# A hybrid S5/GLA decoder layer: other wait points for PE's first pairs, a written-out PE loop, and small moves on four engines

## The chip, the cores and the metric

The kernel runs on one core of a Trainium2 chip. The metric is the time of one execution in device microseconds (us). A core has five engines that run their own instruction streams side by side and wait for each other on semaphores: PE (TensorE, matrix products into PSUM), DVE (VectorE), ACT (ScalarE), POOL (GpSimd) and SP (SyncE, here a DMA queue). ACT issues DMAs as well. PSUM has eight banks of 512 fp32 columns.

## The reference

One layer of a decoder over 2048 prompt tokens and 8 x 4 new tokens, in fp32, width 1024:

```python
h = rmsnorm(x, g_mix)
z = h @ w_in          # u | q | k | v | r | a_low | gate_s5 | gate_gla
y5 = s5_mixer(u, ...)                       # 32 groups, 64 complex states
z5 = gelu(y5); o5 = z5 * sigmoid(z5 @ w_s5_glu)
og = gla_mixer(q, k, v, log_sigmoid(a_low @ w_gate_up + b_gate) / 16, ...)
og = rmsnorm_per_head(og) * g_gla_norm * silu(r)
m = sigmoid(gate_s5) * (o5 @ w_s5_br) + sigmoid(gate_gla) * (og @ w_gla_br)
x = x + m @ w_out
x = x + relu(rmsnorm(x, g_ffn) @ w_ff1) ** 2 @ w_ff2
y = rmsnorm(x, g_final)
```

## The kernel before

Activations lie feature-major: a tile is 128 features by all tokens of a half. The tokens are cut in two halves; the first has 1024 prompt tokens in two blocks of 512 columns, the second 1024 prompt tokens and all 32 new ones in three blocks of 352. Each half runs the whole layer, one after the other.

To keep fp32 accuracy, every operand is split in a high and a low part, and each product is three matmuls (`three`, lines 589 to 591): high x high, high weight x low, low weight x high. Weights come in blocks of 128 x 512 (four 128 x 128 pieces). SP loads a block into one of 2 raw buffers when POOL has split the block two earlier; POOL makes the high and low part (`split`, lines 571 and 573) in one of 4 places, in order 0, 1, 2, 3, when PE has finished with that place (`w_used`); PE waits for `w_split` of the place. SP's queue also carries, between the loads, the constants (`first_loads`) and the gates that come back from DRAM.

PE writes a product either in a set of banks (set 0: banks 0 to 2, set 1: banks 3 to 5) or, for the jobs in between ("dense": keys, inputs, gates, branch products), block by block in banks 6 and 7 by turns. Before PE starts a tile in a set it waits for the set's reader (`set_free`, semaphores `set0_read` and `set1_read`). In a stage such as the output product or the feed-forward part, `tile_pair` makes a tile in set 0 and then one in set 1. The first two tiles of a stage go through `first_pair` instead (from line 653): the right-hand tiles k = 0 to 7 are just being made by ACT and DVE (`split_ready` counts DVE's low parts), so the pair goes over k in the outer loop and over the two sets in the inner one:

```python
for s in range(2):
    set_free(half, s, stage, 0)
for n in range(2):
    for s in range(2):
        pe.wait_ge(w_split[2 * s + n], it + 1)
    for q in range(4):
```

It is used for the queries (`SP_X`), the output product (`SP_MG`) and the feed-forward part (`SP_H2`), in each half.

The start: ACT squares the eight input tiles as they land, DVE adds the squares (line 1650), PE sums them over the features (`row_sums`, line 644), ACT makes the root, DVE scales, ACT and DVE split, and PE's first pair begins.

After the values' products PE transposes each value tile (`values`, lines 722 and 724) and ACT copies it out (`values_out`, lines 1292 and 1294). Between `values(2)` and `values(3)` stands a whole gate tile ("gs", 0). Then the GLA chunks begin with `gla_keys` (line 735), which waits for all four value tiles.

In the branches (`branches` on DVE and ACT) PE makes GLA branch tiles ("bg"), the S5 gate's products ("glu") and the S5 branch ("bs") in the order of `D_JOBS`. DVE multiplies each "bg" block by its gate (`gla_block`), which frees the bank, and makes the low part of the S5 output z (`z_low`), for which it waits for ACT's rounded high part. The gates were stored in DRAM and come back on SP's queue (`gla_gate_back`, line 476; semaphores `gg_landed`). PE waits for all four low parts before "glu".

The feed-forward part has 8 groups of "up" and "down" products; three turns of a register loop on PE (line 1094), ACT and DVE make groups 2 to 7. In the second half `ff_last` makes the last group's final four tiles block by block (4 tiles x 12 matmuls a block), so that the final norm can start on block 0: DVE adds each piece to the residual, ACT squares it, DVE adds squares, PE sums them (`last_sums`, lines 911 and 913, one tile into the second piece of the next block), ACT makes the root (`root_block`, lines 1551 and 1554), DVE scales eight pieces (`scale_block`, line 2372) and SP stores four tiles at a time (lines 556 and 558).

## Time and profile before

| | |
|---|---|
| time, median of 3 runs | 2885.11 us (2884.95 to 2885.32) |
| the profiled execution's own time | 2883.77 us |
| its span | 2881.6 us |
| PE busy | 2816.3 us (98%) |
| PE weight loads busy | 2532.0 us (88%) |
| DVE busy | 1323.2 us (46%) |
| POOL busy | 1168.8 us (41%) |
| ACT busy | 502.3 us (17%) |

The span is what the trace covers; the execution's own time has some 2 us around it. Lines such as L589 are lines of the kernel before; most DVE operations have the line of a helper (L1650), so they are told apart by their tiles: `f_` names a fp32 view of a region, `r_` the rounded view of the same memory, `ps` is PSUM. Matmuls overlap, and their ends are modelled.

### The profile page before, as it was taken

The page shows a single profiled execution, that of the slowest core. Times are in us where ns is not written, and L with a number is a line of the kernel's source. Part 1 is how long each engine was busy: PE and PEld are TensorE (multiplying, and loading weights), DVE is VectorE, ACT ScalarE, POOL GpSimd, SP SyncE. Part 2 cuts the span into 40 slices and gives each one's busy share as a digit, 9 for nine tenths or more (in the row PEclk, how much of TensorE's full clock was granted, in tenths as well). Part 3 has the DMA queues.
Part 4 walks back from the last instruction along what each step waited for, and adds up shares of the span by engine and source line. Part 5 has one row for each costly group of instructions (what it writes and reads, how often), then busy time and mean ns, then how long its engine had stood idle before and what let it go on. Part 6 is the DMA issues. An engine that isn't in the chain of part 4 may idle for free.

```text
span 2881.6 us, 40391 instructions
## 1 busy us (share of the span) xinstructions
PE 2816.3 (98%) x16170; PEld 2532.0 (88%) x16170; DVE 1323.2 (46%) x2039; ACT 502.3 (17%) x731; POOL 1168.8 (41%) x917
## 2 busy tenths in 40 slices
PE   6999999999999999999999999999999999999997
PEld 4778888887888888888899999999999999999997
DVE  7845657364433333234723556666444223332235
ACT  3222221412100000001222223142120000000002
POOL 4433432544544444444444332244444443344441
PEclk9999999999999999999999999999999999999999
DMA  4333244531111111113113333563211111111112
GB/s 144 118 96 88 67 132 154 186 99 52 48 48 48 49 48 48 48 48 108 48 54 123 76 84 100 169 211 100 71 42 47 48 45 45 48 45 48 45 48 75
DMA packets 122999, 230.48 MB, mean 80 GB/s; under 512 B 15280, under 2 KB 43728, under 8 KB 122704
## 3 DMA queue, kind: packets, MB, share of 16 engines
q1 hardware_dynamic: 79312, 150.16, 17.3%
q10 hardware_dynamic: 43520, 77.83, 8.5%
q8 instruction: 137, 2.24, 0.3%
q14 instruction: 30, 0.25, 0.0%
HBM read 183.85 MB, written 44.09 MB: 79 GB/s over the span
## 4 chain that ended last, share of the span: by engine, by line
PE 94%; DVE 3%; ACT 1%; DVEq 1%; issue 1%; ACTq 0%; DMA 0%
PE ps L589 29%; PE ps L591 29%; PE ps L590 29%; PE ps L753 1%; PE ps L838 1%; PE ps L871 1%; PE ps L784 0%; DVE f_h L1650 0%; PE ps L865 0%; DVE f_m L1650 0%; DVE f_g L1650 0%; DVE f_z L2372 0%; PE ps L762 0%; DMA s_constants<-f_m 0%; PE ps L644 0%
## 5 line engine op out<-in xcount | busy, mean ns | idle before, releaser
L571 POOL TENSOR_TENSOR w_hi<-w_raw,zero 128x512 fp32r<-128x512 f32 x456 | 536.0, 1175 | 1607.8 <-PE ps L591 1593.7
L589 PE MATMUL ps<-r_h,w_hi 128*128 128x352 f32 (+1 forms) x2352 | 817.7, 348 | 14.2 <-DVE r_h L1650 5.5
L591 PE MATMUL ps<-r_h,w_lo 128*128 128x352 f32 (+1 forms) x2352 | 816.0, 347 | 0.0
L590 PE MATMUL ps<-r_o,w_hi 128*128 128x352 f32 (+1 forms) x1968 | 679.5, 345 | 0.0
L573 POOL TENSOR_TENSOR w_lo<-w_raw,w_hi 128x512 fp32r<-128x512 f32 x456 | 634.7, 1392 | 64.8
L589 PE MATMUL ps<-r_z,w_hi 128*128 128x352 f32 (+1 forms) x1440 | 516.4, 359 | 3.4 <-issue 3.4
L591 PE MATMUL ps<-r_z,w_lo 128*128 128x352 f32 (+1 forms) x1440 | 514.5, 357 | 0.0
L590 PE MATMUL ps<-r_h,w_hi 128*128 128x512 f32 (+1 forms) x1352 | 499.3, 369 | 0.0
L589 PEld LDWEIGHTS ps<-r_h,w_hi 128*128 128x128 f32 x2352 | 442.9, 188 | 52.5 <-issue 14.5
L591 PEld LDWEIGHTS ps<-r_h,w_lo 128*128 128x128 f32 x2352 | 442.9, 188 | 32.2
L590 PE MATMUL ps<-r_m,w_hi 128*128 128x352 f32 (+1 forms) x1240 | 421.2, 340 | 0.0
L590 PEld LDWEIGHTS ps<-r_o,w_hi 128*128 128x128 f32 x1968 | 370.9, 188 | 28.5 <-issue 0.5
L589 PEld LDWEIGHTS ps<-r_z,w_hi 128*128 128x128 f32 x1440 | 271.6, 189 | 36.7 <-issue 6.9
L591 PEld LDWEIGHTS ps<-r_z,w_lo 128*128 128x128 f32 x1440 | 271.6, 189 | 27.7
L590 PEld LDWEIGHTS ps<-r_h,w_hi 128*128 128x128 f32 x1352 | 255.3, 189 | 39.2 <-issue 0.5
L2236 DVE SCALAR_TENSOR_TENSOR f_g<-ps,f_e 128x1024 f32<-128x1024 f32 (+1 forms) x64 | 79.4, 1241 | 394.0 <-PE ps L591 394.0
L1650 DVE TENSOR_TENSOR f_z<-f_z,ps 128x1056 f32<-128x1056 f32 (+1 forms) x104 | 103.8, 999 | 311.7 <-PE ps L591 311.6
L590 PEld LDWEIGHTS ps<-r_m,w_hi 128*128 128x128 f32 x1240 | 233.0, 188 | 13.6
L1650 DVE TENSOR_TENSOR f_h<-f_h,ps 128x1024 f32<-128x1024 f32 (+1 forms) x102 | 108.4, 1063 | 293.3 <-PE ps L591 291.8
L1650 DVE TENSOR_TENSOR f_g<-f_g 128x1024 f32<-128x1024 f32 (+2 forms) x110 | 191.8, 1756 | 8.4
L591 PE MATMUL ps<-r_m,w_lo 128*128 128x512 f32 x384 | 151.6, 395 | 0.0
L589 PE MATMUL ps<-r_m,w_hi 128*128 128x512 f32 x384 | 150.5, 392 | 0.1
(323 smaller groups left out, 2398.4 us busy)
## 6 DMA issues: line engine op xcount, KB each, us to landing
w_raw<-wpack SPq DMA_DIRECT2D x456, 256.0 KB, 2.6
f_z<-s_constants ACTq DMA_DIRECT2D x16, 514.0 KB, 4.9
f_h<-s_constants ACTq DMA_DIRECT2D x16, 514.0 KB, 5.3
f_h<-xT ACTq DMA_DIRECT2D x16, 512.0 KB, 4.2
gate_s_scratch<-f_m ACTq DMA_DIRECT2D x8, 528.0 KB, 3.5
gate_gla_scratch<-f_m ACTq DMA_DIRECT2D x8, 528.0 KB, 3.5
f_z<-gate_s_scratch SPq DMA_DIRECT2D x8, 528.0 KB, 5.4
f_o<-xT ACTq DMA_DIRECT2D x4, 1040.0 KB, 7.8
```

The costliest lines, as they stand in the source:

```text
L571: pool.tensor_tensor(w_hi[:, s, :], raw, zero[:, :].to_broadcast([P, WB]), ALU.subtract)
L573: pool.tensor_tensor(w_lo[:, s, :], raw, w_hi[:, s, :].bitcast(F32), ALU.subtract).then_inc(w_split[s], 1)
L589: pe.matmul(out, wh, h, start=first, stop=False)
L590: pe.matmul(out, wh, l, start=False, stop=False)
L591: return pe.matmul(out, wl, h, start=False, stop=last)
L753: last = pe.matmul(ps[0:L - LEVELS[l], 2 * (col // 512) + h % 2, col % 512:col % 512 + L // 2], fa[rows, at:at + L - LEVELS[l]], right, st ...
L838: last = pe.matmul(ps[64 * g:64 * g + 64, 4 + t % 2, q * uc:(q + 1) * uc], fv(QKV[half] + C_SLOT[r] + c0 + 64 * g, 64), fv(WORK[half] + (t ...
L871: last = pe.matmul(out(t, g), fa[rows(g), at(t) + c0:at(t) + c0 + P], fa[rows(g), st:st + yc], start=False, stop=q == 1)
L1650: return dve.tensor_tensor(out, a, b, op)
L2236: dve.scalar_tensor_tensor(cols(half, r), psum_cols(half, q % 2), 0.0, cols(half, ft(half, E_NORM)), ALU.max, ALU.mult).then_inc(set_read[ ...
```

## The change

- `first_pair`, for `SP_H2` in both halves and for `SP_X` in the second: PE waits for set 0 alone, takes k = 0 to 3 in set 0, then waits for set 1 and takes k = 0 to 3 there; k = 4 to 7 as before.
- PE's loop over the feed-forward groups is a Python loop: its instructions are written out.
- `ff_last` waits for set 1 only ahead of its fourth tile; `last_sums` of a block comes after the first piece of the next block, ACT's `root_block` ahead of that block's squares; DVE scales the block before in two halves, behind its adds of pieces 2 and 3; SP stores two tiles at a time.
- POOL waits for the first sums (`ssum_ready`) before the second of the first four splits.
- PE makes one block of ("gs", 0), then `values(3)`, then the other blocks; ACT follows.
- DVE makes two GLA tiles, then the S5 low parts by turns with the blocks of the next two; PE waits for the low parts of "glu" and "bs" one by one.

```diff
             for s in range(RING):
+                if s == 1:
+                    pool.wait_ge(ssum_ready, 1)
                 split(s, 0)
...
             def first_pair(half, stage, it, split, hi, lo, between=None):
-                for s in range(2):
+                alone = split == SP_H2 or (split == SP_X and half > 0)
+                for s in range(1 if alone else 2):
                     set_free(half, s, stage, 0)
                 for n in range(2):
+                    if alone and n == 0:
+                        for s in range(2):
+                            if s:
+                                set_free(half, s, stage, 0)
+                            pe.wait_ge(w_split[2 * s], it + 1)
+                            for k in range(4):
+                                pe.wait_ge(split_ready, half * SP_ALL + split + k + 1)
+                                last = tiles_of(half, s, k, KT_D, w_hi[:, 2 * s, k * P:(k + 1) * P],
+                                                w_lo[:, 2 * s, k * P:(k + 1) * P], hi, lo)
+                            last.then_inc(w_used[2 * s], 1)
+                        if between:
+                            between()
+                        continue
...
-                for s in range(2):
-                    set_free(half, s, "ff", ff_set(g, "down") + LAST // 2)
+                set_free(half, 0, "ff", ff_set(g, "down") + LAST // 2)
...
                         if b == 0:
+                            if x == RING - 1:
+                                set_free(half, 1, "ff", ff_set(g, "down") + LAST // 2)
...
-                        if b and x == 1:
+                        if b and x == 0:
                             last_sums(half, b - 1)
...
-                dense_tile(half, ("gs", 0), x_hi, x_lo)
+                dense_block(half, ("gs", 0), 0, x_hi, x_lo)
                 values(half, 3)
+                for b in range(1, NB[half]):
+                    dense_block(half, ("gs", 0), b, x_hi, x_lo)
...
+                    elif m == 0:
+                        dense(half, (kind, 0), 0, 0, z_hi, z_lo, SP_Z5 if kind == "glu" else SP_O5)
+                        for b in range(1, NB[half]):
+                            dense_block(half, (kind, 0), b, z_hi, z_lo)
                     else:
-                        if m == 0:
-                            pe.wait_ge(split_ready, half * SP_ALL + (SP_Z5 if kind == "glu" else SP_O5) + KT_S)
                         dense_tile(half, (kind, m), z_hi, z_lo)
...
-                with pe.Fori(0, FF_GROUPS // 2 - 1) as i:
+                for i in range(FF_GROUPS // 2 - 1):
...
                 for b, (c0, cn) in enumerate(BLK[half]):
+                    if b:
+                        root_block(b - 1)
                     for x in range(RING):
...
-                        if b and x == 1:
-                            root_block(b - 1)
...
                 gla_branch(0)
+                gla_branch(1)
                 z_low(0)
-                gla_branch(1)
-                z_low(1)
-                z_low(2)
-                gla_branch(2)
-                z_low(3)
-                gla_branch(3)
+                for m in (2, 3):
+                    dve.wait_ge(gg_landed[m], (half + 1) * 16)
+                    gla_block(m, 0)
+                    z_low(2 * m - 3)
+                    for b in range(1, NB[half]):
+                        gla_block(m, b)
+                    if m == 2:
+                        z_low(2)
...
-                        last.then_inc(ssum_ready, 1)
-                        if b:
-                            scale_block(b - 1)
-                    scale_block(NB[half] - 1)
+                            if x == RING - 1:
+                                last.then_inc(ssum_ready, 1)
+                            if b and x >= 2:
+                                scale_block(b - 1, range((x - 2) * RING, (x - 1) * RING))
+                    scale_block(NB[half] - 1, range(KT_D))
```

How the order moves, at three places. PE at the start of the feed-forward part's first pair in the first half (`r_m`, `r_h_57`: the output product's right-hand sides; `r_z`, `r_o`: high and low part of the feed-forward input; in brackets the semaphores waited for). Before:

```order
L589 MATMUL ps<-r_m,w_hi 128x512
L590 MATMUL ps<-r_h_57,w_hi 128x512
L591 MATMUL ps<-r_m,w_lo 128x512
L589 MATMUL ps<-r_z,w_hi 128x512 [waits w_split2,w_split0,split_ready,set1_read,set0_read]
L590 MATMUL ps<-r_o,w_hi 128x512
```

Now:

```order
L592 MATMUL ps<-r_m,w_hi 128x512
L593 MATMUL ps<-r_h_57,w_hi 128x512
L594 MATMUL ps<-r_m,w_lo 128x512
L592 MATMUL ps<-r_z,w_hi 128x512 [waits split_ready,w_split0,set0_read]
L593 MATMUL ps<-r_o,w_hi 128x512
```

The waits for place 2 and for set 1 have left the first product; they stand at the product 24 matmuls later.

DVE in the second half's branches (`f_o<-f_g,ps` and `f_o<-f_o,ps`: GLA blocks, three to a tile; `r_m<-f_h_49,r_h_57`: an S5 low part). Before:

```order
L1650 TENSOR_TENSOR f_o<-f_g,ps 128x352 x3
L1650 TENSOR_TENSOR r_m<-f_h_49,r_h_57 128x1056
L1650 TENSOR_TENSOR f_o<-f_o,ps 128x352 x3
L1650 TENSOR_TENSOR r_m<-f_h_49,r_h_57 128x1056 x2
L1650 TENSOR_TENSOR f_o<-f_o,ps 128x352 x3
L1650 TENSOR_TENSOR r_m<-f_h_49,r_h_57 128x1056
L1650 TENSOR_TENSOR f_o<-f_o,ps 128x352 x3
```

Now:

```order
L1675 TENSOR_TENSOR f_o<-f_g,ps 128x352 x3
L1675 TENSOR_TENSOR f_o<-f_o,ps 128x352 x3
L1675 TENSOR_TENSOR r_m<-f_h_49,r_h_57 128x1056
L1675 TENSOR_TENSOR f_o<-f_o,ps 128x352
L1675 TENSOR_TENSOR r_m<-f_h_49,r_h_57 128x1056
L1675 TENSOR_TENSOR f_o<-f_o,ps 128x352 x2
L1675 TENSOR_TENSOR r_m<-f_h_49,r_h_57 128x1056
L1675 TENSOR_TENSOR f_o<-f_o,ps 128x352
L1675 TENSOR_TENSOR r_m<-f_h_49,r_h_57 128x1056
L1675 TENSOR_TENSOR f_o<-f_o,ps 128x352 x2
```

Six GLA blocks now stand ahead of the first low part, and each later low part behind a single block or a pair.

DVE at the end, from the second block's last piece on (`f_z<-f_z,ps`: a piece's add; `f_h_49`: squares added; `f_z<-f_z,vec,f_e`: a scaled piece). Before:

```order
L2372 SCALAR_TENSOR_TENSOR f_z<-f_z,vec,f_e 128x352 x8
L1650 TENSOR_TENSOR f_z<-f_z,ps 128x352 x2
L1650 TENSOR_TENSOR f_h_49<-f_h_49 128x352
L1650 TENSOR_TENSOR f_z<-f_z,ps 128x352
L1650 TENSOR_TENSOR f_h_49<-f_h_49 128x352
L1650 TENSOR_TENSOR f_z<-f_z,ps 128x352
L1650 TENSOR_TENSOR f_h_49<-f_h_49 128x352
L2372 SCALAR_TENSOR_TENSOR f_z<-f_z,vec,f_e 128x352 x16
```

Now:

```order
L2401 SCALAR_TENSOR_TENSOR f_z<-f_z,vec,f_e 128x352 x4
L1675 TENSOR_TENSOR f_z<-f_z,ps 128x352 x2
L1675 TENSOR_TENSOR f_h_49<-f_h_49 128x352
L1675 TENSOR_TENSOR f_z<-f_z,ps 128x352
L1675 TENSOR_TENSOR f_h_49<-f_h_49 128x352
L2401 SCALAR_TENSOR_TENSOR f_z<-f_z,vec,f_e 128x352 x4
L1675 TENSOR_TENSOR f_z<-f_z,ps 128x352
L1675 TENSOR_TENSOR f_h_49<-f_h_49 128x352
L2401 SCALAR_TENSOR_TENSOR f_z<-f_z,vec,f_e 128x352 x12
```

Eight of the last sixteen scalings have moved ahead, four before the last piece's add and four behind its squares' sum. In all, PE's order has 10302 rows before and 14092 now.

## Rows read from the trace of the kernel before

**Rows 1.** The page's first part: busy us (share of the span) x instructions

```profile
PE 2816.3 (98%) x16170; PEld 2532.0 (88%) x16170; DVE 1323.2 (46%) x2039; ACT 502.3 (17%) x731; POOL 1168.8 (41%) x917
```

**Rows 2.** Waits of PE: engine, line, whom; us in total, times, longest

```profile
PE ps L589 <- issue: 8.8, 6, 2.0
...
PE ps L735 <- ACT f_z L1292: 1.4, 1, 1.4
PE ps L735 <- ACT f_e L1294: 1.3, 1, 1.3
```

**Rows 3.** Timeline of PE, loop turns, second half: start, us, operation [idle before <-releaser]

```profile
2397.86 0.32 PE L590 MATMUL ps<-r_m,w_hi 128*128 128x352 f32 x1
2398.01 0.32 PE L591 MATMUL ps<-r_h,w_lo 128*128 128x352 f32 x1
2400.06 0.43 PE L589 MATMUL ps<-r_h,w_hi 128*128 128x352 f32 x1 [1.72 <-issue]
...
2585.59 0.42 PE L589 MATMUL ps<-r_h,w_hi 128*128 128x352 f32 x1 [0.93 <-issue]
```

**Rows 4.** The chain that ended last, first 32 us: start, us, engine and line

```profile
12.71 1.23 DVE f_h L1650
...
20.18 2.14 DVE f_h L1650
...
22.45 3.77 PE ps L644 x4
...
31.66 0.76 PE ps L589
```

**Rows 5.** Timeline of ACT: the last input tile's square

```profile
17.26 1.06 ACT L1178 ACTIVATE f_h<-f_h 128x1024 f32<-128x1024 f32 x1 [0.17 <-DMA f_h<-xT]
```

**Rows 6.** Groups by line, POOL: busy us, mean ns of one | idle before

```profile
L573 POOL TENSOR_TENSOR w_lo<-w_raw,w_hi 128x512 fp32r<-128x512 f32 x456 | 634.7, 1392 | 64.8
L571 POOL TENSOR_TENSOR w_hi<-w_raw,zero 128x512 fp32r<-128x512 f32 x456 | 536.0, 1175 | 1607.8 <-PE ps L591 1593.7 <-DMA w_raw<-wpack 13.9
```

**Rows 7.** Timeline of PE: first products of three first pairs

```profile
710.90 0.47 PE L589 MATMUL ps<-r_z,w_hi 128*128 128x512 f32 x1 [1.36 <-issue]
...
1425.99 0.40 PE L589 MATMUL ps<-r_z,w_hi 128*128 128x352 f32 x1 [2.04 <-issue]
...
2119.24 0.40 PE L589 MATMUL ps<-r_h,w_hi 128*128 128x352 f32 x1 [1.40 <-issue]
```

**Rows 8.** Timeline of DVE: reads of set 0 and set 1 before the first pair

```profile
698.51 1.22 DVE L1650 TENSOR_TENSOR f_h<-f_h,ps 128x1024 f32<-128x1024 f32 x1 [6.43 <-PE ps L591]
...
709.58 1.22 DVE L1650 TENSOR_TENSOR f_h<-f_h,ps 128x1024 f32<-128x1024 f32 x1 [6.42 <-PE ps L591]
```

**Rows 9.** Timeline of PE: first product of the last group's four tiles

```profile
2840.69 0.40 PE L589 MATMUL ps<-r_o,w_hi 128*128 128x352 f32 x1 [1.39 <-issue]
```

**Rows 10.** Timeline of ACT: copies of the fourth value tile, first half

```profile
218.19 1.08 ACT L1292 ACTIVATE f_z<-ps 128x512 f32<-128x512 f32 x2 [0.47 <-PE ps L722]
```

**Rows 11.** Timelines of DVE and PE in the second half's branches

```profile
1914.51 1.26 DVE L1650 TENSOR_TENSOR r_m<-f_h,r_h 128x1056 fp32r<-128x1056 f32 x1 [3.63 <-ACT r_h L1496]
...
1916.25 0.43 PE L589 MATMUL ps<-r_h,w_hi 128*128 128x352 f32 x1 [2.09 <-DVE f_o L1650]
...
1923.49 0.43 PE L589 MATMUL ps<-r_h,w_hi 128*128 128x352 f32 x1 [1.23 <-DVE f_o L1650]
```

**Rows 12.** The gates' tile, 1913 to 1915 us: issues, and us from issue to landing

```profile
L476 SPq DMA_DIRECT2D f_o<-gate_gla_scratch x2: 430/430/430, 1913.4 to 1913.8; - x2
...
DMA to landing us min/median/max: 6.1/6.5/7.0
```

**Rows 13.** Timeline of DVE: the last scalings

```profile
2868.68 8.12 DVE L2372 SCALAR_TENSOR_TENSOR f_z<-f_z,vec,f_e 128x352 f32<-128x352 f32 x16
```

**Rows 14.** Busy time from 2872 to 2880: PE, PEld, DVE, ACT, POOL, clock, DMA, GB/s

```profile
2872.00:2880.00 8.00, 0.00 (x0) 0.00 (x0) 4.78 (x10) 0.70 (x2) 0.00 (x0) 0.50 1.03 345
```

More of the change, by code:

```diff
@@ L550, in _ @@
             for b, (c0, cn) in enumerate(BLK[half]):
-                for k in range(0, KT_D, RING):
-                    sp.wait_ge(y_ready, KT_D + 2 * b + k // RING + 1)
-                    y = fv(X_HI[half] + k * W, RING * W).rearrange("p (k n) -> p k n", n=W)
+                for k in range(0, KT_D, 2):
+                    sp.wait_ge(y_ready, KT_D + 4 * b + k // 2 + 1)
+                    y = fv(X_HI[half] + k * W, 2 * W).rearrange("p (k n) -> p k n", n=W)
                     own = min(cn, N - c0)
-                    out = [yT[h, :, k * N:(k + RING) * N].rearrange("p (k n) -> p k n", n=N) for h in range(HALVES)]
+                    out = [yT[h, :, k * N:(k + 2) * N].rearrange("p (k n) -> p k n", n=N) for h in range(HALVES)]
                     sp.dma_start(out[half][:, :, c0:c0 + own], y[:, :, c0:c0 + own]).then_inc(y_stored, 16)
@@ L1633, in _ @@
                 exps(half, 1)
-                for b in range(NB[half]):
+                gate_out(half, 0, 0)
+                values_out(half, 3)
+                for b in range(1, NB[half]):
                     gate_out(half, 0, b)
-                values_out(half, 3)
                 gla(half)
@@ L1643, in _ @@
             act.wait_ge(s5dec_stored, 32)
-            act.wait_ge(y_stored, 16 * (KT_D + 2 * NB[1] + 2))
+            act.wait_ge(y_stored, 16 * (KT_D + 4 * NB[1] + 4))
         @block.vector
@@ L2189, in branches @@
                 gla_branch(0)
+                gla_branch(1)
                 z_low(0)
-                gla_branch(1)
-                z_low(1)
-                z_low(2)
-                gla_branch(2)
-                z_low(3)
-                gla_branch(3)
+                for m in (2, 3):
+                    dve.wait_ge(gg_landed[m], (half + 1) * 16)
+                    gla_block(m, 0)
+                    z_low(2 * m - 3)
+                    for b in range(1, NB[half]):
+                        gla_block(m, b)
+                    if m == 2:
+                        z_low(2)
                 for m in range(KT_S):
@@ L2365, in last_square, with scale_block @@
                                   ALU.add)
-                    def scale_block(b):
+                    def scale_block(b, tiles):
                         c0, cn = BLK[half][b]
                         dve.wait_ge(root_ready, NORM[half]["y"] + b + 1)
-                        for k in range(KT_D):
+                        for k in tiles:
                             y = ft(half, X_HI[half], k)[:, c0:c0 + cn]
@@ L2373, in scale_block @@
                                                             ft(half, E_NORM)[:, c0:c0 + cn], ALU.mult, ALU.mult)
-                            if k % RING == RING - 1:
+                            if k % 2:
                                 last.then_inc(y_ready, 1)
```

## The prediction

> **What bounds the kernel now.** Start with the busy table: PE (TensorE) works 2816.3 of 2881.6 us [rows 1]. No other engine comes near, so time is won only where PE stands idle, 65 us in all. Next read who makes PE wait: of that list the change touches the entry "issue" with 8.8 us in 6 places, two waits for ACT at the GLA keys (1.4 and 1.3 us) [rows 2], and the starts and the end that follow below. "Issue" says only that no releaser was seen; the timeline around each place tells what it was. In the list and in the timeline a matmul's end is modelled: in 352-column blocks matmuls start every 0.16 us (2397.86, 2398.01) and show 0.32 [rows 3], so an idle time printed in brackets is about 0.16 us shorter than what PE lost. I add 0.16 to each PE gap between matmuls of the three-product kind.
>
> **The start (GpSimd's wait).** DVE adds eight squared tiles. The third add runs 1.23 us; the last, beside GpSimd's weight splits, 2.14, and PE's first sums follow it at 22.45 [rows 4]. With three of the four splits held until the sums are there, five adds from 12.71 at about 1.3 each would be through at 19.2. ACT's last square ends at 17.26 + 1.06 = 18.32 [rows 5], and one add of 1.23 behind it ends at 19.6. So the sums come 22.32 - 19.6 = 2.7 us sooner. The fourth weight load now waits for the second split, so 256 KB less stand before the input's last tiles, which then come a little sooner; I take **3.0 us**, from 2.7 as the lower bound without that. What is late next: three splits of 1.18 + 1.39 = 2.57 us by the means [rows 6] run from 19.3 and end by 27.0; PE's pair needs the places 0 and 2, so two of the held splits, 24.5. PE's first product, now at 31.66 [rows 4], would be at 28.7. Four us of room. SP's queue is held too: behind the fourth load stand the constants, masks and S5 tables (`first_loads`), which go out some 5 us later; PE asks for the constants before the same product, and the rest is used only after the input's eight tiles.
>
> **First pairs.** PE waits for both bank sets before the first product: idle 1.36, 2.04 and 1.40 us [rows 7]. The second set's reader is DVE's add, 709.58 + 1.22 = 710.80, and PE goes on at 710.90; the first set was read from 698.51 on [rows 8]. The change asks for set 1 only after half of set 0's product, 4 tiles x 2 blocks x 3 matmuls x 0.23 = 5.5 us later (4 x 3 x 3 x 0.16 = 5.8 in the second half), when that add is long done. Low parts of tiles 0 to 3 are ready long before, and the number of products is the same. Gain 4.80 + 3 x 0.16 = **5.3 us**. It costs nothing as long as place 2's split is done 5.5 us after place 0's; GpSimd does them in the order 0, 1, 2, and had both before.
>
> **PE's loop written out.** In the second half the loop's two turns cost 1.72 and 0.93 us [rows 3]; in the first half no turn is among the six. Gain 2.65 + 2 x 0.16 = **3.0 us**. No operation is added or taken away; what stands against the term is the first rival below.
>
> **Last group.** Before its last four tiles PE waits for both sets, 1.39 us [rows 9]; set 1 is then needed only by the fourth tile, 3 x 12 x 0.16 = 5.8 us on. Gain **1.5 us**. DVE is behind on the first of these blocks, but has caught up when PE asks for the first sums.
>
> **Values before the rest of the gate.** PE's keys wait 1.37 and 1.31 us (1.4 and 1.3 in the list [rows 2]) for ACT's copies of the fourth value tile, which begin at 218.19 and end 1.1 us later [rows 10]. With one gate block before these transposes and the others behind, the copies have at least 3.8 us of PE work to hide under. Gain **2.7 us**. ACT's key copy then comes behind the last gate block, but PE has a gate product between.
>
> **S5's low parts in turn.** DVE's first low part stands 3.63 us waiting for ACT's rounded tile, and the GLA blocks behind it in the queue hold PE's banks: PE loses 2.09 and, at the next such place, 1.23 us [rows 11]. With two GLA tiles first, and then a low part behind each one's first block, DVE never waits long: 2.09 + 1.23 + 0.32 = 3.6 us. But the wait is not gone: the third gate tile's load is issued at 1913.4 and the fourth's at 1913.8, and they land 6.1 and 7.0 us later [rows 12], the third at 1919.5 at the earliest. PE, no longer held, finishes that tile's first block about 1917.7 (the held block would have begun at 1916.25 - 2.09 - 0.16 = 1914.0, and a block is 12 x 0.16 = 1.92 us) and needs its bank again at 1919.8; DVE's product ends near 1920.2. I take 0.6 off: **3.0 us** (1.4 if the load is a us later and DVE chases it, 3.6 at best). In the first half PE did not wait here, and the new order leaves it so. The wait per tile instead of four changes nothing: the last low part is done before PE is there.
>
> **The tail.** Roots move up by a tile, and block 1's scaling goes in two halves behind DVE's adds of tiles 2 and 3. Good: in the profile, DVE scales sixteen pieces without a break from 2868.68, 8.12 us [rows 13], the stores of both blocks leave together, and the DMA engines are full from 2872 to 2880 at 345 GB/s [rows 14], over 3 us past DVE's last piece. With block 1's stores earlier, and two-tile stores (0.35 MB, 1.0 us at that rate), the end follows the last piece by about 1.2 us less. Bad: four scalings, 4 x 0.51 = 2.0 us, now stand before DVE's last add, and the last root comes later by an estimated 0.7 us; PE also waits a little for the middle block's sums. Net **0.5 us**, between -0.7 and 1.2.
>
> **Sum.** 3.0 + 5.3 + 3.0 + 1.5 + 2.7 + 3.0 + 0.5 = 19.0 us. The profiled execution took 2883.77 us (span 2881.6), so 2864.8; the median of the runs shown, 2885.11, is 1.34 above it. I forecast 2866.1 for the median.
>
> **Rivals.**
> - *Written-out code starves PE* (slower). The PE program grows from 10302 to 14092 rows of the order; if PE met a fetch stall where it now enters new code, each costing what a turn costs (1.72 us [rows 3]), at each of the 24 up and down parts that the loops held, that is 41 us: 2866.1 + 41 = 2907. From 15 such stalls on (25 us) the change is slower by more than 0.2%. For it: only the loop's turns show such idle time. Against it: over half of PE's time is spent in straight code already, and the six places of "issue" are three first pairs, two turns and the last group [rows 2, 3, 7, 9]. 3%. The Trainium skill, Runtime: NRT & Kernel Launch, Instruction fetch mechanics, says that an engine's instructions are fetched ahead in sequence, and that a taken branch to a place not yet fetched stalls. By that rule the turns' gain is kept whole and this rival doesn't occur; the trace agrees in that the straight parts show no such row, and differs in that the first half's turns, branches too, show none either.
> - *The start gives its gain back.* The held splits run on beside DVE's later steps, and DVE's operations of that kind take 1.23 alone and 2.14 beside a split [rows 4]. If the splits slip by 2 us, they meet the first scaling and low part, and the 3.0 go: 2869. The Trainium skill, SBUF — State Buffer, Who interferes with whom, has GpSimd and DVE exclude each other for a whole instruction; by it such a meeting costs either one up to the other's full length. 10%.
> - *The next wait is close behind.* The gaps at the first pairs, the last group and the S5 branch close only in part, because DVE and ACT, which now feed an earlier PE, are themselves the limit; half of 5.3 + 1.5 + 3.0 is lost: 2871. For it: PE's second wait in the S5 branch follows the first by 7 us [rows 11]. Against it: at the first pairs DVE has only one add left. 12%.
> - *The change doesn't do it.* "Issue" at the first pairs and the last group is not the set's wait but a cost of the place itself (a code change, the weights' split), and stays: 2866.1 + 6.8 = 2873. Against it: PE goes on 0.10 us after DVE's add [rows 7, 8]. 4%.
>
> **How the numbers follow.** My forecast has 71%, these four 29%. The sum's upper bounds (3.3, 5.5, 3.4, 1.6, 2.7, 3.6, 1.2) give 21.3 us, that is 2864; rounding up for the restart of PE after each closed gap, 2862. The lower ones (2.0, 4.0, 2.0, 1.0, 2.0, 1.4, 0) give 12.4 and 2873, which takes in three of the rivals. A measurement of this kernel tells about 0.2%, 5.8 us, from no change. All cases but the written-out stream, and some mishap that I don't see, lie beyond it: faster 92%, same 4%, slower 4%.
>
> **What would show it.** In the changed profile: DVE's adds all near 1.23 us and PE's first sums near 19.5; no idle row at the three first pairs, the loop's turns and the last group; PE's keys without a wait; in the second half's GLA branch at most one wait, of under 1 us, whose cause is the gate's load. At the end the DMA engines should not be full when DVE's last piece is done, and the last root should come later against PE's last product. I am wrong if new "issue" rows stand inside the feed-forward part, or if PE waits for a split or for low parts after the first pairs' first set.

## The result, and the profile after

The changed kernel takes **2861.53 us** (median of four executions, 2860.50 to 2865.04) beside 2885.22 us for the kernel before: ratio 0.9918, 95% interval 0.9901 to 0.9935. It is faster, by more than the 19.0 us of the sum: the median is half a microsecond below the range of 2862 to 2873. Five further executions of the same kernel have a median of 2863.11 us (below), inside the range, so the half microsecond itself is within the spread. The profiled execution took 2860.5 us with a span of 2858.6, 23.0 us shorter than the span before.

The first part of the changed kernel's page answers to [rows 1]: PE has the same 16170 matmuls in 5.4 us less of busy time, so a part of the gain is not idle time at all: some 3 us of it are the lower clock below.

```profile
PE 2810.9 (98%) x16170; PEld 2529.5 (88%) x16170; DVE 1324.5 (46%) x2039; ACT 502.5 (18%) x731; POOL 1165.6 (41%) x917
```

All waits of PE in the changed kernel (line, whom it waited for, us in total, times, longest). Against [rows 2] the entry "issue" and the two waits at the keys are gone. L592 is now what L589 was, L753 what L735 was.

```profile
PE ps L647 <- DVE f_h L1675: 19.4, 1, 19.4
PE ps L592 <- DVE r_h L1675: 6.8, 1, 6.8
PE ps L883 <- DVE f_m L2130: 3.3, 2, 2.5
PE ps L929 <- DVE f_h L1675: 2.8, 2, 2.3
PE ps L592 <- DVE f_o L1675: 1.3, 1, 1.3
PE ps L771 <- ACT khT L1375: 1.3, 1, 1.3
PE ps L740 <- ACT f_z L1287: 1.0, 1, 1.0
PE ps L706 <- DVE f_z L1882: 1.0, 1, 1.0
PE ps L883 <- DVE f_o L2130: 0.7, 1, 0.7
```

PE's timeline in the changed kernel at the six places of [rows 3, 7, 9] (first pairs, loop turns, last group): the product starts with no idle time in brackets.

```profile
704.64 0.39 PE L592 MATMUL ps<-r_z,w_hi 128*128 128x512 f32 x1
...
1417.02 0.32 PE L592 MATMUL ps<-r_z,w_hi 128*128 128x352 f32 x1
...
2101.90 0.32 PE L592 MATMUL ps<-r_h,w_hi 128*128 128x352 f32 x1
...
2380.73 0.32 PE L592 MATMUL ps<-r_h,w_hi 128*128 128x352 f32 x1
2565.05 0.32 PE L592 MATMUL ps<-r_h,w_hi 128*128 128x352 f32 x1
...
2818.49 0.32 PE L592 MATMUL ps<-r_o,w_hi 128*128 128x352 f32 x1
```

PE does the same matmuls in nearly the same order, so the gain can be followed: take the start of one matmul before, less its start after. At the second first pair that is 1425.99 - 1417.02 = 8.97 us so far. By place, in us, each read once the difference is steady again behind the place:

| place | forecast | profiled |
|---|---|---|
| start, at the first product | 3.0 | 31.66 - 29.94 = 1.7 |
| values, both halves | 2.7 | 1.6 + 1.5 = 3.1 |
| PE at a lower clock near 434 us | none | 1.5 |
| three first pairs | 5.3 | 1.6 + 2.3 + 1.6 = 5.5 |
| PE at a lower clock behind the second | none | 1.5 |
| loop, with 0.4 in the first half | 3.0 | 0.4 + 2.0 + 1.2 = 3.6 |
| S5's low parts | 3.0 | 2.3 + 1.4 = 3.7 |
| last group | 1.5 | 1.6 |
| tail | 0.5 | 0.7 |
| rest | | 0.1 |

The two lower clocks are seen in the windows of the kernel before (columns: PE, PEld, DVE, ACT, POOL busy, granted clock, DMA share, GB/s). PE is busy throughout. The first window stands at 0.50, which is the level of 1.2 GHz and not of 2.4; the second, at 0.66 in the mean, reaches beyond such a stretch on both sides:

```profile
1427.50:1430.50 3.00, 3.00 (x12) 3.00 (x12) 3.00 (x3) 2.27 (x3) 0.00 (x0) 0.50 0.58 161
433.00:438.00 5.00, 5.00 (x41) 4.46 (x42) 0.18 (x1) 0.60 (x1) 0.00 (x0) 0.66 0.16 34
```

The same work in the changed kernel:

```profile
1417.00:1421.00 4.00, 4.00 (x26) 3.98 (x25) 4.00 (x3) 0.93 (x1) 2.85 (x2) 1.00 0.14 53
431.00:435.00 4.00, 4.00 (x41) 3.36 (x41) 1.84 (x7) 0.60 (x1) 0.00 (x0) 1.00 0.48 153
```

At the start the sums come at 19.38 us, close to the 19.5 of the prediction, but the first product only 1.7 us sooner. DVE's timeline in the changed kernel shows the step between them: the angle steps, which the prediction doesn't name, take from 19.15 to 27.74 us.

```profile
19.15 0.17 DVE L1724 TENSOR_SCALAR f_o<-f_o 128x16 f32<-128x16 f32 x1
...
19.47 0.91 DVE L1675 TENSOR_TENSOR f_o<-f_o 128x16 f32<-128x16 f32 x1
20.31 2.64 DVE L1729 TENSOR_SCALAR f_e<-f_e 128x16 f32<-128x16 f32 x8
23.03 1.24 DVE L1732 TENSOR_SCALAR f_e<-f_e 128x144 f32<-128x144 f32 x1
24.34 0.23 DVE L1734 TENSOR_SCALAR f_e<-f_e 128x144 f32<-128x144 f32 x1
24.66 2.78 DVE L1737 SCALAR_TENSOR_TENSOR f_e<-f_e 128x144 f32<-128x144 f32 x3
...
27.66 1.41 DVE L2293 SCALAR_TENSOR_TENSOR f_h<-f_h,vec,f_g 128x512 f32<-128x512 f32 x2
```

GpSimd's held splits at that time, in its timeline:

```profile
22.91 1.26 POOL L573 TENSOR_TENSOR w_lo<-w_raw,w_hi 128x512 fp32r<-128x512 f32 x1
24.44 1.04 POOL L571 TENSOR_TENSOR w_hi<-w_raw,zero 128x512 fp32r<-128x512 f32 x1 [0.27 <-DMA w_raw<-wpack]
25.62 1.27 POOL L573 TENSOR_TENSOR w_lo<-w_raw,w_hi 128x512 fp32r<-128x512 f32 x1
```

DVE's operation at 23.03 ends at 24.27, just behind GpSimd's at 22.91 + 1.26 = 24.17; the next one falls into GpSimd's pause and takes 0.23. The Trainium skill, SBUF — State Buffer, Who interferes with whom, lets one of the two engines hold the shared pair of ports for a whole instruction; these rows agree. ACT's root was ready by 25.18 + 1.06 = 26.24:

```profile
25.18 1.06 ACT L1167 ACTIVATE f_g<-f_g 128x1024 f32<-128x1024 f32 x1
```

### The profile page after: what moved, and what is told of

Read it like the earlier page. It is cut to its first block, busy times and chain, and to the rows that moved or that the text cites. A ratio compares the mean times of both kernels' runs of the same rounds, so it can differ in the third digit from the quotient of the medians.

```text
span 2858.6 us, 40302 instructions
## 1 busy us (share of the span) xinstructions
PE 2810.9 (98%) x16170; PEld 2529.5 (88%) x16170; DVE 1324.5 (46%) x2039; ACT 502.5 (18%) x731; POOL 1165.6 (41%) x917
## 4 chain that ended last, share of the span: by engine, by line
PE 95%; DVE 3%; DMA 1%; DVEq 1%; ACT 0%; issue 0%; ACTq 0%
PE ps L594 29%; PE ps L592 29%; PE ps L593 29%; PE ps L771 1%; PE ps L856 1%; PE ps L889 1%; PE ps L883 1%; PE ps L802 0%; PE ps L780 0%; DMA s_constants<-f_m 0%; DVE f_m L1675 0%; PE ps L813 0%; DMA f_h<-xT 0%; DVE f_g L1675 0%; DVE f_h L1675 0%; PE ps L987 0%
## 5 line engine op out<-in xcount | busy, mean ns | idle before, releaser
L592 PE MATMUL ps<-r_h,w_hi 128*128 128x352 f32 (+1 forms) x2352 | 817.5, 348 | 8.2 <-DVE r_h L1675 6.8
L592 PE MATMUL ps<-r_z,w_hi 128*128 128x352 f32 (+1 forms) x1440 | 515.6, 358 | 0.0
L592 PEld LDWEIGHTS ps<-r_h,w_hi 128*128 128x128 f32 x2352 | 442.9, 188 | 45.2 <-issue 11.0
L592 PEld LDWEIGHTS ps<-r_z,w_hi 128*128 128x128 f32 x1440 | 271.0, 188 | 32.6 <-issue 2.7
L592 PE MATMUL ps<-r_m,w_hi 128*128 128x512 f32 x384 | 150.3, 391 | 0.0
```

The source lines that it names most:

```text
L592: pe.matmul(out, wh, h, start=first, stop=False)
```

## The experiments

Theory after the result: the gain is the sum of closed gaps, plus the end of a lower clock that followed one of them, less 1.35 us lost where the held splits meet DVE's angle steps. Single executions of one program differ by several us here (2860.50 to 2865.04 above), so medians of four or five tell little about 1 us. What follows is read from the start of the same matmul in two traces; "the changed kernel" is the profile above. Together with the two profiles above, 18 profiles are compared.

### The start

```diff
 for s in range(RING):
-    if s == 1:
-        pool.wait_ge(ssum_ready, 1)
     split(s, 0)
```

> The changed kernel with GpSimd's one new wait (for the first row sums) taken out; all else stays. Theory: the wait buys the first sums 3.07 us (22.45 to 19.38 us) and costs 1.35 us of them, because the three held splits now run beside DVE's angle steps (8.6 us instead of 3.2). Without it the first sums return to 22.3 to 22.6 us, the angle steps to 3.2 us, the first product to 31.5 to 31.8 us (29.94 with the wait), and the time rises by 1.7 us. Rival, the earlier sums come from something else (arrival of the input): the sums stay near 19.4 us without the wait, the first product comes near 28.6 us, and the time falls by about 1.3 us.

Measured: median 2864.3 us; first sums at 22.56, first product at 31.77. DVE's angle steps, in this kernel's timeline:

```profile
22.64 0.17 DVE L1673 TENSOR_TENSOR f_o<-f_o 128x16 f32<-128x16 f32 x1
22.74 0.70 DVE L1727 TENSOR_SCALAR f_e<-f_e 128x16 f32<-128x16 f32 x8
23.52 0.23 DVE L1730 TENSOR_SCALAR f_e<-f_e 128x144 f32<-128x144 f32 x1
...
24.15 1.07 DVE L1735 SCALAR_TENSOR_TENSOR f_e<-f_e 128x144 f32<-128x144 f32 x3
...
29.48 1.42 DVE L2291 SCALAR_TENSOR_TENSOR f_h<-f_h,vec,f_g 128x512 f32<-128x512 f32 x2 [3.95 <-ACT f_g L1165]
```

The same operations without splits beside them: 0.70 us for eight that took 2.64, and DVE waits 3.95 us for the root. The wait moves the sums by 3.2 us and the first product by 1.8; the sums' gain is the wait's.

```diff
-    trig_angles()
     norm_root(NORM[0]["x"], A_G)
 ...
     for k in range(1, KT_D + 1):
         input_tile(0, k)
+    trig_angles()
```

> The changed kernel with GpSimd's wait kept and DVE's angle steps moved from between the first sums and the first scaling to behind the eight input tiles (ScalarE's sine, which reads them, comes later still). Theory: the angle steps beside the held splits were the only thing that gave back part of the earlier sums; the first scaling starts at the end of ScalarE's root, near 26.3 us (27.66 before this edit), the first product near 28.6 us (29.94), and the time falls by 1.3 us. Rival, the start gives its gain back in whatever DVE does beside the splits: the first scaling and the first low part grow by what the angle steps lost, the first product stays between 29.5 and 30.0 us and the time does not move.

Measured: median 2862.22 us. With the sums at 19.59, the first scaling starts when the root is done, and the first product comes at 29.18, 0.76 us sooner:

```profile
26.52 1.79 DVE L2292 SCALAR_TENSOR_TENSOR f_h<-f_h,vec,f_g 128x512 f32<-128x512 f32 x2 [7.07 <-ACT f_g L1167]
```

Measured from the sums, 0.97 of the 1.35 us come back; the other 0.38 go to the rival, since the scaling beside the last held split takes 1.79 instead of 1.41. The median doesn't show it: PE waits 0.4 us more for the S5 kernel's tables (near 145 us) and 1.1 us at a gate (below). Whether the later place of the angle steps causes the first of these isn't shown: the wait is 0.98 us in the changed kernel's profile and 1.55 in a second one of the same kernel, against 1.39 here.

The third is both edits together:

> Both edits at once: no wait of GpSimd, and the angle steps behind the input tiles. Theory: with the sums at 22.3 to 22.6 us the root ends near 29.3 us and the angle steps were done long before it, so that their place is worth nothing here: first product 31.4 to 31.8 us, as with the angle steps in their old place. The wait is then worth 3.0 us with the angle steps out of the way and 1.7 us with them in the way. Rival, the angle steps cost by themselves and not through the splits: the first product comes 1.3 us earlier here too, near 30.3 us.

Measured: first product at 31.77 us, the same as with the angle steps in their old place, so they cost nothing by themselves. (One execution, 2867.69 us; behind the product PE loses 2 us more at the S5 kernel's tables, and some to longer stretches of lower clock near 35, 155 and 1775 us.)

```diff
-    if s == 1:
+    if s == 2:
         pool.wait_ge(ssum_ready, 1)
```

> The changed kernel with GpSimd's wait for the first row sums ahead of its third split instead of its second. The second then runs from 6.0 to 8.5 us, ahead of VectorE's first add (9.8 us), and only two splits (4.8 us) are left to run beside the angle steps. Theory: the sums stay at 19.4 us; the angle steps do some 1.8 us of their 3.2 us of work while the splits run (8.6 us beside them against 3.2 alone) and end near 25.6 us, ahead of ScalarE's root (26.2); the first scaling starts at the root's end, 26.3 us, and the first product comes at 28.6 us (29.94), so that PE is 1.3 us earlier. Rival, the shared work is GpSimd's own queue and not the place: the angle steps still end behind 27 us and PE gains less than 0.4 us.

Measured: sums at 20.15 us, 0.77 later than in the changed kernel. All squares of the input end later here; over the thirteen profiles with the wait the sums lie between 19.0 and 20.3. The first product comes at 29.36, 9.21 us behind the sums instead of 10.56: 1.35 us are back, all of what the splits took. DVE in this kernel:

```profile
21.08 2.64 DVE L1729 TENSOR_SCALAR f_e<-f_e 128x16 f32<-128x16 f32 x8
...
25.42 1.07 DVE L1737 SCALAR_TENSOR_TENSOR f_e<-f_e 128x144 f32<-128x144 f32 x3
...
27.07 1.41 DVE L2293 SCALAR_TENSOR_TENSOR f_h<-f_h,vec,f_g 128x512 f32<-128x512 f32 x2 [0.27 <-ACT f_g L1167]
```

The first eight still meet a split, the last three don't, and DVE is ready 0.27 us ahead of the root. Median 2862.6 us.

### The first pairs, and the clock behind a gap

```diff
-alone = split == SP_H2 or (split == SP_X and half > 0)
+alone = False
```

> The changed kernel with the first pairs at three places (the feed-forward's in both halves, the query's in the second) put back to turns between the two bank sets. Theory: PE's gaps of 1.36, 2.04 and 1.40 us come back, with the lesser ones beside them 5.3 us in all, and PE's steps before and behind those places are as in the changed kernel, so that the time rises by 5.3 us. The term was put at 5.3; the two profiles differed by 7.2 us at the three places, because in the kernel before the granted clock also stood at 0.5 for 3.4 us behind the longest gap, which cost another 1.9. If that fall belongs to the gap it comes back too, at about 1417 us, and the time rises by 7.2 us. Rival, the fall is a matter of the single run: the gaps come back without it. Second rival, the gaps were shifted work that comes back elsewhere: the time rises by under 3 us.

Measured: median 2870.09 us, 8.6 above the changed kernel's. PE's entry "issue" is back with 4.8 us in 3 places; PE loses 1.6, 2.3 and 1.6 us there, and another 1.5 behind the second, where the granted clock is at 0.50 again. The window in this kernel, behind its gap:

```profile
1423.00:1426.00 3.00, 3.00 (x11) 3.00 (x12) 3.00 (x2) 0.91 (x1) 0.94 (x1) 0.50 0.29 85
```

Sum 7.0 of the 7.2 expected. Another 1.9 us of this profile stand at 429 to 436 us, again at 0.50, and 1.2 us behind PE's last sums. Whether either fall belongs to the change one profile can't tell; three more bear on it, two of the kernel before, and one with the pairs put back:

> The kernel before, profiled again. Theory: the granted clock falls to 0.5 again behind the gap of 2.04 us at 1426 us, for about 3.4 us, and costs PE some 1.6 to 1.9 us there; near 434 us it may or may not fall. Rival, the fall at 1427 us was chance: it is absent here, and the gap costs its 2.04 us alone.

> The kernel before, a third profile. Theory: as in the second, a granted clock of 0.5 behind the gap at 1426 us. Rival: none there.

> The changed kernel with the first pairs put back, a second profile. Theory: a granted clock of 0.5 behind the gap near 1422 us again, with or without one near 432 us. Rival: none there.

Measured: 2887.24, 2884.73 and 2870.99 us. Each has the fall behind the gap. The windows, of the second profile of the kernel before, then of the third, then of the pairs put back:

```profile
1427.50:1430.00 2.50, 2.50 (x10) 2.50 (x10) 2.50 (x3) 1.41 (x2) 0.00 (x0) 0.51 0.39 118
```

```profile
1427.50:1430.00 2.50, 2.50 (x10) 2.50 (x9) 2.50 (x3) 1.31 (x2) 0.04 (x1) 0.50 0.40 110
```

```profile
1423.00:1426.00 3.00, 3.00 (x11) 3.00 (x12) 3.00 (x2) 1.03 (x2) 0.82 (x1) 0.50 0.31 87
```

So the fall at the second first pair stands in all five profiles that have the gap, and in none of the thirteen that haven't: it belongs to the gap, and its 1.5 us to the change. The other, near 434 us, follows a wait of 2.53 us at the S5 rows, the same in all 18 (L883 in the list above), that no edit here touches. It stands in 10 of the 18, among them the changed kernel run again (below), so one program does both. That the kernel before has it in three of three leaves open whether the change makes it rarer. A third such stretch, near 1490 us, comes in five of the 18, for 1.5 us each time.

Nor does every gap of that length bring a fall. In the second profile of the kernel before PE's wait in the S5 branch [rows 11] is followed by one too, and costs 1.5 us more than the wait:

```profile
1918.35 0.66 PE L589 MATMUL ps<-r_h,w_hi 128*128 128x352 f32 x1 [2.22 <-DVE f_o L1650]
```

```profile
1918.50:1921.00 2.50, 2.50 (x9) 2.50 (x10) 0.22 (x1) 2.47 (x4) 0.00 (x0) 0.50 0.91 311
```

The same wait is 2.09 and 2.25 us in the other two profiles of that kernel, and 2.35 in the run with the low parts put back (below), and no fall follows it there: one in four, where the first pair has five in five.

### The loop, the S5 low parts, the values, the last group

```diff
-for i in range(FF_GROUPS // 2 - 1):
+with pe.Fori(0, FF_GROUPS // 2 - 1) as i:
```

> The changed kernel with PE's feed-forward loop as a counted loop again. Theory: the turns cost what the kernel before shows, two of 1.72 and 0.93 us in the second half with what follows them and 0.4 us in the first: 3.0 to 3.6 us more, in PE's idle time put down to nothing that the profile shows, and no other change. Rival, the written-out code costs PE something all along (waiting for its instructions) that the gain hides: with the loop back the stretches between the turns run faster and the time rises by less than 1.5 us.

Measured: median 2865.40 us. PE's waits show "issue" with 2.8 us in 2 places, and PE loses 1.8 and 1.6 us at the two turns, none in the first half, and nothing between the turns: 3.4 us. (In the kernel before, a turn of the first half lost 0.4.) Timeline of PE:

```profile
2382.80 0.43 PE L592 MATMUL ps<-r_h,w_hi 128*128 128x352 f32 x1 [1.51 <-issue]
```

```profile
2568.69 0.42 PE L592 MATMUL ps<-r_h,w_hi 128*128 128x352 f32 x1 [1.29 <-issue]
```

The written-out code costs nothing that could be seen. The Trainium skill, Runtime: NRT & Kernel Launch, Instruction fetch mechanics, names a taken branch to a place not yet fetched as what stalls; in this run the second half's turns show idle time, the first half's turns and the straight code none.

```diff
 gla_branch(0)
+z_low(0)
 gla_branch(1)
-z_low(0)
-for m in (2, 3):
...
+z_low(1)
+z_low(2)
+gla_branch(2)
+z_low(3)
+gla_branch(3)
```

(with PE's one wait for four low parts, as before.)

> The changed kernel with VectorE's order in the branches and PE's waits for the S5 low parts put back. Theory: PE's waits of 2.09 and 1.23 us come back in the second half (near 1905 and 1912 us) with 0.2 to 0.4 us in the first half, so that PE is 3.0 to 3.7 us later behind them, and the time rises by as much. Rival, the gates' transfers: VectorE's new order waits for the third gate, and in the changed kernel that landing ends a wait of VectorE's of 1.45 us, so that PE is released by it with under 0.5 us to spare; put back, the order hides this, and the rise is under 2 us.

Measured: median 2866.12 us; PE loses 2.6 and 1.3 us, 3.9 in all and a little over what was expected, and nothing in the first half. Its rows answer to [rows 11]:

```profile
1904.28 0.43 PE L592 MATMUL ps<-r_h,w_hi 128*128 128x352 f32 x1 [2.35 <-DVE f_o L1673]
1911.52 0.43 PE L592 MATMUL ps<-r_h,w_hi 128*128 128x352 f32 x1 [1.22 <-DVE f_o L1673]
```

```diff
-dense_block(half, ("gs", 0), 0, x_hi, x_lo)
+dense_tile(half, ("gs", 0), x_hi, x_lo)
 values(half, 3)
-for b in range(1, NB[half]):
-    dense_block(half, ("gs", 0), b, x_hi, x_lo)
```

(and ACT's copies likewise.)

> The changed kernel with the last values behind the whole first gate tile on PE and ScalarE again, as before the change. Theory: each half loses 1.3 to 1.7 us at the values (near 217 and 925 us of the first half's and second half's values), PE waiting for ScalarE's copies, and the time rises by 2.7 to 3.0 us. Rival, VectorE's first differences and products set the pace there and not the values' copies: the loss is under 1 us in each half.

Measured: median 2866.88 us; PE's waits at L753 come back with 1.4 and 1.3 us, and PE is 1.6 and 1.5 us later behind them: 3.1, as between the two profiles above. That is a little over what was expected, and over the term's 2.7, which took the printed waits as they stand.

```diff
-set_free(half, 0, "ff", ff_set(g, "down") + LAST // 2)
+for s in range(2):
+    set_free(half, s, "ff", ff_set(g, "down") + LAST // 2)
```

> The changed kernel with PE's wait for the second bank set put back ahead of the last group's first tile. Theory: PE's gap of 1.39 us ahead of that group comes back, PE is 1.4 to 1.7 us later behind it, and the end is as much later. Rival, the wait for the second set only moves the gap three tiles on in the changed kernel: PE loses under 0.5 us.

Measured: the gap is back with 1.40 us, and PE is 1.6 us later behind it. (One execution, 2868.26 us; lower clocks cost it 2.7 us from 429 to 436 and 1.5 near 1491.)

### The gate's transfer, the tail, and all together

DVE's timeline in the changed kernel shows what lies behind the S5 gain: its block of the third gate tile starts when the gate's transfer lands, not when PE is done. The two gates' loads in the changed kernel answer to [rows 12]:

```profile
L476 SPq DMA_DIRECT2D f_o<-gate_gla_scratch x2: 430/431/432, 1901.6 to 1902.1; - x2
...
DMA to landing us min/median/max: 5.4/5.9/6.4
```

```profile
1907.11 0.52 DVE L1675 TENSOR_TENSOR f_o<-f_o,ps 128x352 f32<-128x352 f32 x1 [1.45 <-DMA f_o<-gate_gla_scratch]
```

```diff
     for j in range(J): ...
+    gla_gate_back(half, 2)
     sp.wait_ge(yrow3_stored, (half + 1) * 16 * J)
```

(and the same gate is skipped at its later place.)

> The changed kernel with one transfer of SyncE's queue moved: the third GLA gate is fetched between the stores of the last S5 tile and the wait for them, not behind the fetch of that tile and one weight block. Theory: in the changed kernel the landing of that gate ends VectorE's wait ahead of its block (1.45 us near 1907 us), with PE held 0, 0.41 and 1.08 us behind it in three runs; the queue stands idle there for over 1 us, so that the gate lands some 4 us earlier, VectorE's block waits for PE alone, and PE has no wait there in any run: 0 to 1.1 us. Rival, the transfer delays the last S5 tile, whose parts PE then waits for: 0.5 to 2 us more of waiting behind 1908 us, and slower.

Measured: median 2861.37 us. The block now waits 0.30 us, for PE, and PE doesn't wait near 1908 us. (A wait of 1.33 us near 1950 us, later in these branches, stands in all 18 profiles.) DVE's row:

```profile
1906.54 0.52 DVE L1678 TENSOR_TENSOR f_o<-f_o,ps 128x352 f32<-128x352 f32 x1 [0.30 <-PE ps L597]
```

Twelve profiles have the change's order without this edit. PE isn't held in five, the changed kernel's among them, and is held by 0.21 to 1.08 us in seven, by 0.51 in the changed kernel run again. In the five the third gate lands 5.1 to 5.6 us after its issue, in the seven 5.6 to 6.6. So the wait that the prediction expected is there, at 0 to 1.1 us, and it follows the gate's landing.

```diff
-if b and x >= 2:
-    scale_block(b - 1, range((x - 2) * RING, (x - 1) * RING))
+if b:
+    scale_block(b - 1, range(KT_D))   # behind all four x
```

> The changed kernel with the early root of the last tiles and the stores of two tiles kept, but DVE's eight scalings of one column block all behind the next block's last sum, as in the kernel before. Theory: in the changed kernel DVE's add of the last piece waits 1.2 us behind four scalings (2843.9 to 2845.9 us) while PE's last sums wait 2.34 us and DVE itself idles 2.00 us for the last root; with the scalings behind, the last square starts 1.2 us earlier, the idle 2.00 us is filled by the scalings, and DVE's last scaling ends 1.0 us earlier: the time falls by 0.8 to 1.2 us. Rival, the stores set the end: DVE ends earlier but the sixteen scaled pieces then leave in a row, and the time falls by less than 0.3 us or not at all.

In the changed kernel DVE goes like this at the end (four scalings, the last add, four more, then 2.00 us idle):

```profile
2843.91 2.06 DVE L2401 SCALAR_TENSOR_TENSOR f_z<-f_z,vec,f_e 128x352 f32<-128x352 f32 x4
2845.90 0.51 DVE L1675 TENSOR_TENSOR f_z<-f_z,ps 128x352 f32<-128x352 f32 x1
...
2851.01 4.06 DVE L2401 SCALAR_TENSOR_TENSOR f_z<-f_z,vec,f_e 128x352 f32<-128x352 f32 x8 [2.00 <-ACT f_e L1578]
```

Measured with the scalings behind: PE's wait for the last sums falls from 2.34 to 1.23 us, and the sixteen scalings run without a break, as in [rows 13]:

```profile
2848.62 8.12 DVE L2401 SCALAR_TENSOR_TENSOR f_z<-f_z,vec,f_e 128x352 f32<-128x352 f32 x16
```

PE's wait of 0.42 us for the middle block's sums, in the 2.8 us of the list above, is gone too. Against the changed kernel PE was 3.45 us late ahead of these sums (stretches of lower clock and the gate's wait), 1.68 us late at the last sums, and the span ends 2.10 us late: the tail is 1.35 us shorter, a little more than expected. 0.4 us of PE's 1.8 are lost again behind PE's last sums; that the stores, which now leave with less between them, are the cause isn't shown. The median, 2863.81 us, doesn't show the gain. The tail's other parts, the earlier root and the stores of two tiles, were not put back one by one.

The wait ahead of the third split, the early gate and this edit, in one kernel, beside the changed kernel itself once more, on one chip:

> Three edits on the changed kernel at once: the wait ahead of the third split, the early gate, and the scalings of one block behind the last sum of the next. Theory: the places are far apart and PE carries each gain on: 1.3 us at the start, 0 to 1.1 us at the gate, 0.8 us at the end, 2.1 to 3.2 us in all, so 2858.5 to 2859.5 us as the median against 2861.5 us. Rival, the gains are taken back by later waits or by the granted clock: 2861 us or more.

> The changed kernel itself once more, for a time beside that of the three edits and for which parts of the trace repeat. Theory: the waits repeat within 0.3 us, and so does the absence of a lower granted clock near 1417 us, where the gap is gone; a lower clock near 434 us comes in some runs and not in others, since the wait in front of it is the same in both kernels, and shifts a run by 1.3 us; the median lies between 2860.5 and 2863 us. Rival, the fall near 434 us is the kernel before's own: it is absent here again.

Measured: 2862.83 us (2858.66 to 2863.52, ratio 0.9918, 0.9905 to 0.9932) against 2863.11 us (2861.31 to 2864.84, ratio 0.9920, 0.9906 to 0.9933). Each edit does its part in the trace: the first product 9.20 us behind the sums, the gate's block waiting 0.30 us for PE, PE's last wait 1.23 us and the tail 1.2 us shorter. But the time of the whole isn't shown to be shorter. The three edits' profile lost 2.7 us near 434 us, that of the changed kernel again 1.4, at the lower clock, and each 1.5 more near 1490 us (windows near 434 us of the three edits, then of the changed kernel again):

```profile
431.00:435.00 4.00, 4.00 (x33) 3.55 (x34) 0.00 (x0) 0.60 (x1) 0.00 (x0) 0.50 0.14 19
```

```profile
431.00:435.00 4.00, 4.00 (x34) 3.40 (x33) 0.55 (x2) 0.60 (x1) 0.00 (x0) 0.57 0.38 84
```

That one program has this stretch in one execution and not in another is the rest of the answer on the 1.5 us near 434 us: they are in the difference of the two profiles, and that they belong to the change isn't shown.

## Why the prediction was wrong in size

The direction, the places, and the forecast's case were right: no fetch stall came, all six places of "issue" closed, the new wait in the S5 branch stayed small. The time was 4.6 us too high, half a microsecond out of the range. That it fell just outside is chance, as the five further executions show; that the sum was too low is not: the places of the change are worth 21.4 us in the profiles and not 19.0. The step that failed is the size put on closed gaps: 7.0 and not 5.3 us at the first pairs, 3.7 and not 3.0 in the S5 branch, 3.6 and not 3.0 at the loop, 3.1 and not 2.7 at the values, against 1.3 too much at the start. Step by step:

- **First pairs: mis-sized.** "Gain 4.80 + 3 x 0.16 = 5.3 us" prices a gap by its length. The three took 5.5 us in the profile, and behind the gap of 2.04 us PE also ran at 0.50 of its clock, another 1.5 us: 7.0, and 7.0 when put back. The sum put this lower clock at nothing without a reason; it stands in the trace of the kernel before.
- **S5's low parts: mis-sized.** "I take 0.6 off: 3.0 us" took DVE's product to end near 1920.2 us, 0.4 us behind PE's need at 1919.8. Against PE's stream, which is 12.15 us earlier there, the gate's load went out 0.4 us later than before, but landed after 5.4 us and not 6.1, and DVE's product ended at 1907.11 + 0.52 = 1907.63, just ahead of PE's block at 1907.68. So nothing came off in the profile: 3.7 us, and 3.9 when put back. In the twelve profiles the wait is 0 to 1.1 us, 0.3 in the mean: the mechanism was right, and the 0.6 within its spread.
- **The start: wrong in its second half.** The sums' 3.0 us were right (3.07 in the profile, 3.2 against the run without the wait). "Four us of room" counted the splits for PE and left out DVE's own steps between the sums and the first scaling. The rival "The start gives its gain back" came half true, by another meeting than it named: not the first scaling but the angle steps were held up, at a price of 1.35 us; the first product gained 1.7.
- **The loop: a little low.** 3.0 forecast, 3.6 in the profile with 0.4 in the first half, 3.4 when put back.
- **Values: a little low.** 2.7 forecast from the printed waits, 3.1 in the profile and when put back.
- **Last group, tail: right.** 1.6 and 0.7 us against 1.5 and 0.5. In the tail both sides were seen: PE's last sums 0.55 us later against the matmuls before them, behind DVE's four scalings, and 1.3 us less from there to the end.
- **A sign that was missed.** "At most one wait, of under 1 us" in the second half's branch: a wait of 1.33 us near 1950 us stands there, in the kernel before as well.
- **The range.** Its upper bounds were those of the gaps alone, 21.3 us. The lower clock of 1.5 us wasn't in it, nor the chance of one more near 434 us, 1.5 us in these two profiles. With these the upper bounds would have given 2861 and not 2864, and the range, rounded as there, have begun near 2859.

That the lower clock at the second first pair needs the gap is shown (five of five against none of thirteen), and that the angle steps are slowed by the splits as well. Why the falls near 434 and 1490 us come in some executions only, and why the S5 branch's gap brought one in one profile of four, is open.

## What to carry to other kernels

Price a gap of PE by its length and by the granted clock behind it, in more than one profile: a fall can come each time or now and then. When work is held back so that it doesn't disturb one step, list every step of the disturbed engine that it will now run beside, small ones too, up to the next that somebody waits for. To judge edits of 1 us where executions differ by several, follow the start of the same instruction through two traces rather than comparing medians.

## What was not expected of the hardware

DVE operations of 16 columns, some 0.1 us each (eight in 0.70), are held until GpSimd's operation in hand is done: 0.91 us for one that took 0.17. Not each one pays: of the eight that took 2.64 us, two took 1.25 and 1.01 and the others 0.16 each, up to three of them in GpSimd's pauses. A gap of 2.02 to 2.04 us was followed by the lower clock in all five profiles that had it, one of 2.09 to 2.35 us elsewhere in one of four, gaps of 1.36 to 1.72 us in none, and a wait of 2.53 us with many small matmuls behind it in 10 of 18.
